# RG-LRU gates as 64x64 quarters in fp32, recurrence gate kept in SBUF, three staging slots for evacuation

## The reference

```python
xh = xc.reshape(B_, N, LRU_HEADS, LRU_HD)          # 8 heads of 64 channels
r = sigmoid(einsum('bnhi,hij->bnhj', xh, wa).reshape(B_, N, W_LRU) + ba)
i = sigmoid(einsum('bnhi,hij->bnhj', xh, wx).reshape(B_, N, W_LRU) + bx)
log_a = (-LRU_C * r) * softplus(-lam)
a = exp(log_a)
b = sqrt(-expm1(2.0 * log_a)) * (i * xc)           # h_t = a_t h_(t-1) + b_t, both directions
```

## Time and profile before

| | us |
|---|---|
| three runs | 788.52, 792.53, 792.26; median 792.26 |
| the profiled execution | 792.91 |
| its span | 790.7 |
| PE busy in the span | 739.8 (94%) |
| DVE, ACT, POOL busy | 526.6, 449.5, 272.5 |
| from gates(0) to gates(19) | 142.37 to 460.12 |
| PE busy in those 317.75 us | 312.90 |
| ACT busy in them | 253.94 |

### The profile page before, as it was taken

The page is one execution under the profiler, slowest core; times in us unless marked ns, Lnnn a source line. Parts: engine busy times, 40 slices in busy tenths (PEclk is TensorE's granted clock), DMA queues, the critical chain, the costliest instruction groups (busy, mean ns, idle before and its releaser), DMA issues.

```text
span 790.7 us, 9934 instructions
## 1 busy us (share of the span) xinstructions
PE 739.8 (94%) x3468; PEld 602.7 (76%) x3468; DVE 526.6 (67%) x811; ACT 449.5 (57%) x743; POOL 272.5 (34%) x321
## 2 busy tenths in 40 slices
PE   3886989999999999999998999899999999999997
PEld 1574767888888887888887877677787888888885
DVE  4377653757998798887995754776646665666522
ACT  4266643699786986787884982234535133534311
POOL 0122335243534274234423345233211134353421
PEclk9796989999999999999999999899999999999999
DMA  8997003334365355345444043254458667968531
GB/s 360 369 325 225 27 28 96 105 97 117 115 182 151 86 157 176 112 141 162 146 130 137 34 127 135 82 160 134 116 194 315 223 205 244 302 202 293 181 116 72
DMA packets 89218, 130.11 MB, mean 165 GB/s; under 512 B 22768, under 2 KB 54128, under 8 KB 87632
## 3 DMA queue, kind: packets, MB, share of 16 engines
q1 hardware_dynamic: 84800, 115.44, 45.1%
q0 software_dynamic: 4368, 14.03, 6.4%
HBM read 91.17 MB, written 38.27 MB: 164 GB/s over the span
## 4 chain that ended last, share of the span: by engine, by line
PE 59%; DVE 14%; issue 7%; ACT 7%; DMA 7%; POOL 4%; SPq 1%; DVEq 0%; ACTq 0%; POOLq 0%
PE bank L1544 19%; PE bank L1546 19%; PE bank L1545 19%; DMA wm<-in_w_mod 3%; DMA pv<-scratch_u 1%; DVE xg L1186 1%; DVE Qb L1301 1%; DVE xc L1129 1%; ACT fbuf L895 1%; DVE spl L1348 1%; POOL xTh L609 1%; ACT bank L878 1%; DVE xTl L1194 1%; DVE Ib L1291 1%; DVE gacc L1129 1%
## 5 line engine op out<-in xcount | busy, mean ns | idle before, releaser
L1544 PE MATMUL bank<-xTh,wh 128*128 128x512 f32 (+1 forms) x592 | 238.2, 402 | 7.2 <-DVE xTl L1194 4.4
L1546 PE MATMUL bank<-xTh,wl 128*128 128x512 f32 (+1 forms) x592 | 231.9, 392 | 0.0
L1545 PE MATMUL bank<-xTl,wh 128*128 128x512 f32 x576 | 227.2, 395 | 0.0
L1544 PEld LDWEIGHTS bank<-xTh,wh 128*128 128x128 f32 x592 | 113.8, 192 | 32.8 <-DVE xTl L1194 6.4
L1546 PEld LDWEIGHTS bank<-xTh,wl 128*128 128x128 f32 x592 | 113.3, 191 | 23.7
L1545 PEld LDWEIGHTS bank<-xTl,wh 128*128 128x128 f32 x576 | 110.2, 191 | 22.6 <-issue 1.2
L1544 PE MATMUL bank<-xTh 128*128 128x512 f32 (+1 forms) x272 | 104.2, 383 | 1.3 <-issue 0.8
L1546 PE MATMUL bank<-xTh,xTl 128*128 128x512 f32 x256 | 99.6, 389 | 0.0
L1545 PE MATMUL bank<-xTl,xTh 128*128 128x512 f32 x256 | 99.6, 389 | 0.0
L911 ACT ACTIVATE ustage<-bank 128x512 f32<-128x512 f32 x56 | 33.1, 592 | 93.0 <-PE bank L1546 76.3
L609 POOL TENSOR_SCALAR sph<-xc 128x512 fp32r<-128x512 f32 (+1 forms) x36 | 27.1, 769 | 121.1 <-PE bank L1546 68.4
(11 more groups left out here) (192 smaller groups left out, 1413.0 us busy)
## 6 DMA issues: line engine op xcount, KB each, us to landing
scratch_u<-ustage SPq DMA_DIRECT2D x72, 256.0 KB, 3.3
wraw<-in_w_in SPq DMA_DIRECT2D x18, 512.0 KB, 4.6
wm<-in_w_mod SPq DMA_DIRECT2D x8, 1024.0 KB, 14.4
xg<-in_x SPq DMA_DIRECT2D x16, 512.0 KB, 9.0
yb<-scratch_y SPq DMA_DIRECT2D x32, 256.0 KB, 3.6
gb<-scratch_u SPq DMA_DIRECT2D x32, 256.0 KB, 5.1
xres<-in_x SPq DMA_DIRECT2D x16, 512.0 KB, 4.7
out<-tout SPq DMA_DIRECT2D x15, 512.0 KB, 3.0
```

The source lines that it names most:

```text
L1544: mm(out, wh_, xh_, start=first, stop=False)
L1545: mm(out, wh_, xl_, start=False, stop=False)
L1546: return mm(out, wl_, xh_, start=False, stop=last)
```

## The change

The gate products are no longer split. `xc` and the raw 64x64 weight blocks (`gwr`, now two buffers) go to PE as fp32, each block a product of its own with 64 rows and 64 columns. Direction d has four: (rows 0-63 to columns 0-63) and (rows 64-127 to columns 64-127) make r; the two blocks of the input gate are written crosswise, rows 0-63 to columns 64-127 and rows 64-127 to columns 0-63. So the input gate's halves are swapped in PSUM, and ACT reads them back with two activations of 64 partitions for each direction. `gates(q+1)` waits for `xc` itself (`s_cv`) and all sigmoids. r is written to a new SBUF tile `rb`, on which exp, tanh and `one_minus_a2` work. `U_SLOTS` is 3. On DVE, `conv(here + 4)` moves from behind the scans of the context step to behind `one_minus_a2` of the next step (s = 1). The splits of `xc` and of the gate weights are gone on POOL and DVE. The weights' high parts stay on ACT as before; `pyo` and `posc2` only change address. `mm` below is one fp32 matmul of the program, which the hardware runs as two instructions.

```diff
-U_SLOTS = 2
+U_SLOTS = 3
...
-        sph = a3.take("sph", [P, 2, CH], f32r)
-        spl = a3.take("spl", [P, 2, CH], f32r)
...
-        gwh = a3.take("gwh", [P, 4, P], f32r)
-        gwl = a3.take("gwl", [P, 4, P], f32r)
-        gwr = a3.take("gwr", [P, 4, 64])
+        gwr = a3.take("gwr", [P, 2, 4, 64])
+        rb = a3.take("rb", [P, 2, CH])
...
             def load_gate_w(t):
-                if t:
-                    pool.wait_ge(s_gwl, 2 * t)
-                g.dma_start(gwr[:], gate_w[t]).then_inc(s_gw, 16)
+                if t >= 2:
+                    pool.wait_ge(s_pg, (NCH + 1) * (t - 1))
+                g.dma_start(gwr[:, t % 2], gate_w[t]).then_inc(s_gw[t % 2], 16)
...
-                if q + 1 < STEPS:
-                    split(q + 1)
...
                 for d in range(2):
-                    r = gr[d][:, 0:n]
-                    a.activation(r, r, ACT.Sigmoid, bias=par_col("lru_ba", 4 * d + t)).then_inc(s_sig, 1)
+                    a.activation(rb[:, d, 0:n], gr[d][:, 0:n], ACT.Sigmoid,
+                                 bias=par_col("lru_ba", 4 * d + t)).then_inc(s_sig, 1)
                 for d in range(2):
                     if q:
                         act.wait_ge(s_st, 2 * (q - 1) + d + 1)
-                    a.activation(Ib[:, d, 0:n], gi_[d][:, 0:n], ACT.Sigmoid,
-                                 bias=par_col("lru_bx", 4 * d + t)).then_inc(s_sig, 1)
+                    for h, other in ((slice(0, 64), slice(64, 128)), (slice(64, 128), slice(0, 64))):
+                        a.activation(Ib[h, d, 0:n], gi_[d][other, 0:n], ACT.Sigmoid,
+                                     bias=par_col("lru_bx", 4 * d + t)[h]).then_inc(s_sig, 1)
...
                 one_minus_a2(q)
-                if q + 1 < STEPS:
-                    split_lo(q + 1)
+                if s == 1:
+                    conv(here + 4)
...
                 if s == 0:
                     conv(here + 3)
-                    conv(here + 4)
...
                 if s == 0:
-                    pe.wait_ge(s_gwl, 2 * t + 2)
-                pe.wait_ge(s_sl, splits_before(q + 1))
+                    pe.wait_ge(s_gw[t % 2], 16 * (t // 2 + 1))
+                pe.wait_ge(s_cv, (NCH + 1) * t + LAST_PIECE[s] + 1)
                 if q:
-                    pe.wait_ge(s_sig, 4 * q)
-                    pe.wait_ge(s_m2, 2 * q)
-                for m in range(4):
-                    d = 0 if s == 0 else m // 2
-                    b = gi_[m // 2] if m % 2 else gr[m // 2]
-                    ins = mm3(b[:, 0:n], gwh[:, m, :], gwl[:, m, :], sph[:, d, 0:n], spl[:, d, 0:n], True, True)
+                    pe.wait_ge(s_sig, 6 * q)
+                w, top, low = gwr[:, t % 2], slice(0, 64), slice(64, 128)
+                for d, c in enumerate(step_chunks(s)):
+                    x = xc_piece(t, c)
+                    mm(gr[d][top, 0:n], w[top, 2 * d], x[top], start=True, stop=True)
+                    mm(gr[d][low, 0:n], w[low, 2 * d], x[low], start=True, stop=True)
+                    mm(gi_[d][low, 0:n], w[top, 2 * d + 1], x[top], start=True, stop=True)
+                    ins = mm(gi_[d][top, 0:n], w[low, 2 * d + 1], x[low], start=True, stop=True)
                 ins.then_inc(s_pg, 1)
```

More of the change, by code:

```diff
@@ L177, in mixer_kernel @@
         Qb = a3.take("Qb", [P, 2, CH])
[L178 to L180 removed]
+        gwr = a3.take("gwr", [P, 2, 4, 64])
+        rb = a3.take("rb", [P, 2, CH])
+        a3.off += 4 * (CH + 2 * 4 * P - 4 * 64)
         MID_BYTES = a3.off - r0 - 4 * (CTX + SEQ)
@@ L201, in mixer_kernel @@
         lsl = past.take("lsl", [P, 2, CH], f32r)
+        pyo = past.take("pyo", [P, CH])
         a4 = Area(mid0, conv0)
@@ L204, in mixer_kernel @@
         ly = a4.take("ly", [P, 2, CH])
-        pyo = a4.take("pyo", [P, CH])
         pdh = a4.take("pdh", [P, CH], f32r)
@@ L238, in mixer_kernel @@
         posr2 = a6.take("posr2", [P, 2, CH])
-        posc2 = a6.take("posc2", [P, CH])
+        posc2 = at("posc2", [P, CH], conv0)
         def col(i, n=1):
@@ L285, in mixer_kernel @@
         s_us = [sem(f"u_stored{b}") for b in range(U_SLOTS)]
-        s_gz, s_gw, s_gwh, s_gwl = sem("gatew_zeroed"), sem("gatew_in"), sem("gatew_hi"), sem("gatew_lo")
+        s_gw = [sem(f"gatew_in{b}") for b in range(2)]
         s_v, s_cv = [sem(f"v_in{b}") for b in range(2)], sem("convolved")
-        s_sh, s_sl, s_pg, s_sig = sem("split_hi"), sem("split_lo"), sem("gates_done"), sem("sigmoids")
+        s_pg, s_sig = sem("gates_done"), sem("sigmoids")
         s_aq, s_exp, s_m2, s_rt = sem("a_and_q"), sem("tanhs"), sem("one_minus_a2"), sem("roots")
@@ L680, in gated_input @@
                 for d, c in enumerate((f, b)):
-                    pool.wait_ge(s_sig, 4 * q + d + 3)
+                    pool.wait_ge(s_sig, 6 * q + 2 * d + 4)
                     I = Ib[:, d, 0:n]
@@ L745, in _ @@
                 here, after = (NCH + 1) * t, (NCH + 1) * (t + 1)
-                if s == NCH and more:
-                    gate_w_hi(t + 1)
                 if s == 0:
                     load_v(here + 4)
-                if q + 1 < STEPS:
-                    split(q + 1)
                 if s == 1 and more:
@@ L931, in decays @@
                     kc = 4 * d + t
-                    act.wait_ge(s_sig, 4 * q + d + 1)
+                    act.wait_ge(s_sig, 6 * q + d + 1)
                     if s == 0 and t or s == 4:
                         act.wait_ge(s_ya, 4 * t if s == 0 else 4 * t + 2)
-                    r = gr[d][:, 0:n]
+                    r = rb[:, d, 0:n]
                     a.activation(Ab[:, d, 0:n], r, ACT.Exp, scale=kn[:, kc:kc + 1]).then_inc(s_aq, 1)
@@ L1248, in _ @@
             lo_group(NCH)
-            def gate_w_lo(t):
-                for i, h in enumerate((slice(0, 64), slice(64, 128))):
-                    dve.wait_ge(s_gwh, 2 * t + i + 1)
-                    v.tensor_tensor(out=gwl[h, :, h], in0=gwr[h], in1=gwh[h, :, h].bitcast(f32),
-                                    op=ALU.subtract).then_inc(s_gwl, 1)
             def conv(p):
@@ L1281, in one_minus_a2 @@
                     dve.wait_ge(s_exp, 2 * q + d + 1)
-                    stt(Qb[:, d, 0:n], Qb[:, d, 0:n], 1.0, gr[d][:, 0:n], ALU.add, ALU.mult).then_inc(s_m2, 1)
+                    stt(Qb[:, d, 0:n], Qb[:, d, 0:n], 1.0, rb[:, d, 0:n], ALU.add, ALU.mult).then_inc(s_m2, 1)
             def scans(q):
@@ L1339, in conv_w_lo @@
                 v.tensor_tensor(out=cwl[:, b], in0=cwraw[:, b], in1=cwh[:, b].bitcast(f32), op=ALU.subtract).then_inc(s_cwlo, 1)
-            def split_lo(q):
-                t, s = divmod(q, NCH + 1)
-                n = CTX if s == 0 else CH
-                pieces = step_chunks(s)[0:1] if s == 0 else step_chunks(s)
-                for d, c in enumerate(pieces):
-                    dve.wait_ge(s_sh, splits_before(q) + d + 1)
-                    v.tensor_tensor(out=spl[:, d, 0:n], in0=xc_piece(t, c), in1=sph[:, d, 0:n].bitcast(f32),
-                                    op=ALU.subtract).then_inc(s_sl, 1)
             w_lo(4)
@@ L1364, in _ @@
             conv(0)
-            gate_w_lo(0)
-            split_lo(0)
             conv(1)
@@ L1373, in _ @@
                         conv(2)
-                if s == NCH and t + 1 < N_LRU:
-                    gate_w_lo(t + 1)
                 for j in convs_in_step(q, 4):
```

25 lines of the change are left out of this document (removed).

## The result

| | before | after |
|---|---|---|
| median of 8 runs each | 791.81 us | 796.67 us (794.22 to 799.64) |
| ratio, 95% interval | | 1.0076 [1.0050, 1.0101] |
| the profiled execution | 792.91 | 799.64 |
| its span | 790.7 | 797.6 |
| from gates(0) to gates(19) | 317.75 | 322.89 |

What follows compares the result with a forecast made beforehand. PE's instruction stream was taken to bound the gate stage. Gates -19.0, edges +8, waits +0.4 and tail +1.2 gave -9.4 us: 792.9 to 783.5, stated as 783; own range 773 to 792, stated range 772 to 798.

Steps and rivals of the forecast that it cites:

- the paragraph on ACT: Gate stage: two more activations a step, 21.6 us against 63.8 us of ACT idle time, costed at nothing.
- ACT takes over the bound: Rival: gates as cheap as forecast, but ACT's 21.6 us do not fit; 6 us of gain lost, 789; 15 in 100.
- the signs that were to show me wrong: PE waiting for `ustage` or sigmoids in many steps, or the time behind step 19 changing by more than 2 us.
- tail: Behind step 19: PE's 4.64 us wait for pooling weights, fetched after a chain through the sigmoids, grows by 1.2 us.
- gates four at once: Gate products: four array quarters run together, 1.72 us for 2.77 a full step, 0.86 for 1.42 a context step; gain 19.0.
- edges: Going into and out of quarters on PE, two a step: 0.4 us a step, 8 us back in all (0 to 14).
- waits ahead of gates(2), gates(12): New PE waits from the moved `conv(here + 4)` and later sigmoids: about 1.4 us in step 1, 0.5 in step 11.
- third slot: Staging: removes ACT waits like the 8.6 us, which cost PE nothing now but pay part of ACT's bill.
- Both bank rivals: Gate quarters: row halves writing one PSUM bank take turns, 830, 13 in 100; row halves never overlap, 876, 4 in 100.
- the rival of dearer edges: Going into and out of quarters costs 0.9 us a step, weights and streams starting anew: +10 us, 793; 8 in 100.
- that of free ones: Rival: the change does all it says and going into and out of quarters costs nothing: 775; no separate chance.
- The holes of steps 9 and 16: PE idle within these steps: step 9 falls from 1.6 to about 0.5 us, step 16 from 3.14 to near 2.7.

Runs made afterwards that it cites:

- e1: Changed kernel with each direction's input gate read by one whole sigmoid, the exchange of halves left out (output not the reference's): 776.26 us, ratio 0.9819.
- e12: Changed kernel with the recurrence gate's sigmoid back in place in PSUM, gates waiting for `one_minus_a2`: 793.92 us, ratio 1.0037.
- e10: As e9, with the recurrence gate's sigmoid in place in PSUM and gates waiting for `one_minus_a2`: 776.64 us, ratio 0.9828.
- e9: Changed kernel with whole input-gate sigmoids, halves of `xc` exchanged by DMA from POOL's queue, `conv(here + 4)` early: 780.15 us, ratio 0.9867.
- e8: As e6, with the recurrence gate in place in PSUM: 785.9 us, ratio 0.9937.
- e6: Changed kernel with whole input-gate sigmoids, halves of `xc` exchanged by DVE copies, `conv(here + 4)` early: 790.8 us, ratio 1.0012.
- e5: Kernel before, with only each input-gate sigmoid cut into two of 64 partitions, no swap: 807.0 us, ratio 1.0209.
- e11: e1 with two staging slots in place of three, exchange of halves also left out: 780.41 us, ratio 0.9872.

## Why the prediction was wrong

**The step that failed is the paragraph on ACT,** "So I cost it at nothing", and the zero was wrong in three ways.
- *The price.* "Two more activations a step are 16 x 1.16 + 4 x 0.75 = 21.6 us". They are 27.1 us (e1). I took a half for another whole one, 0.58 us. But whole ones in a row overlap their neighbour by 0.12 us (length 0.69, 0.57 apart), and halves stand end to end (four in 2.81 us, 0.70 each): 1.70 us a step and not 1.16. The Trainium skill ("ScalarE: Activation LUTs", What ACT_TABLE_LOAD costs) gives the time of an activation of 128 partitions by its columns, and an overlap of about 93 ns between activations in a row. The whole ones here agree (0.12 us); of 64 partitions it says nothing, and the halves don't show the overlap.
- *A second zero,* in the paragraph behind it. "Moving r to SBUF adds no instruction; the exps already cross from PSUM to SBUF. Zero too." The exps start 0.61 us apart on `rb` and 0.57 on PSUM, six such activations a step with the tanh: 4.9 us of ACT (e12 against after), 4.6 (e10 against e9), and with DVE's share, which I had at nothing too, 3 to 6 us of time (e12 against after, e10 against e9, e8 against e6). Together ACT grew by 31.3 us in the stage; 27.1 and 4.9 make 32.0.
- *The consumer.* "Carried from step to step, ACT's debt stays under 2 us, and it may run about 9 us late before the next gates miss a sigmoid ..." ACT's lag rose from 2.0 to 5.8 us in step 5 and 10.8 in step 8. The changed kernel's gates indeed never missed a sigmoid. What ran dry first was another: `cvzl` of a conv unit, on DVE behind `one_minus_a2`, on ACT's tanh. I had asked what PE waits for from ACT by name, and not what stands behind a DVE instruction that waits for ACT. The idle time I offset the debt against (63.8 us) wasn't free either: a late evacuation makes the next conv weights late (7.26 us of ACT's time in step 7), so lateness feeds itself.

The rival "ACT takes over the bound" had the right mechanism, with 6 us and 15 in 100. Of the signs that were to show me wrong, PE's waits for `ustage` or sigmoids in many steps didn't come, though ACT was the cause; the one that came is the tail, changed by more than 2 us. The stated own range of 773 to 792 is also narrower than its terms, whose bounds added end to end give 772 to 799. The halves took 20 us (after against e1), 16 on the kernel before (e5).

**The sum against the runs** (the stage: 322.89 - 303.67 = 19.2 us between after and e1, of which 13.4 are waits of PE, 17.3 against 3.9 us, and 5.8 the lower clock behind them, by PE's busy time of 305.57 against 299.75, 5.75 of it in the stretches of steps 8, 9 and 16). The times of the two profiled executions differ by 26 us and the medians by 20, so single waits of this pair are good to a few us:

| term | forecast | measured |
|---|---|---|
| gates four at once | 1.72 us a full step | 1.72 (turns of 0.43; what the first has more is in the edges) |
| edges | 0.4 us a step | 0.35 |
| waits ahead of gates(2), gates(12) | 1.4, 0.5 | 1.77, 1.08 (0.09 and none in e1) |
| ACT | 0 | 20 us of time |
| third slot | 0 | -15 us in this state, -4 with ACT at ease |
| tail | +1.2 | +3.1 |

- *Both bank rivals are refuted.* Two row halves wrote one bank and one starts 0.01 us behind the other. By the Trainium skill ("TensorEngine Tiling (Array Packing)", Gotcha 1: PSUM Pressure) this shouldn't be. The Trainium skill's "PSUM — Partial Sum Buffer", PSUM bank collisions raise a hardware error, says the same, and beside it that measured collisions were those within one bank and one quadrant of partitions. Here the halves lie in different partitions, and the trace goes with the second. What the prediction calls the "full value" of packing in rows and columns is, on its page, a speedup of 10.6 with 16 tiles.
- *Edges:* 0.35 us, as taken; the rival of dearer edges and that of free ones both fall.
- *Waits:* gates(2) and gates(12) are right in place and near in size, but that is partly luck. The sum gave 0.5 us of it to the halves and 0.9 to the moved piece; the halves cost 1.70 us a step, and without them the moved piece costs 0.09 us at gates(2) (e1). The holes of steps 9 and 16, said to be 0.5 and 2.7, are near that where ACT isn't late (e10: 1.06 and 1.98; e1: 2.29 and 1.54), and 4.05 and 4.30 in the change.
- *Tail:* the chain named (pooling weights) is not the one that showed: in the change the first pooling product has no wait of note, where 5.8 us were forecast. PE waits 3.28 us for ACT's `ustage` and 3.78 for `lq`; with ACT at ease (e1) the pooling wait is 1.29, not 4.64, so the tail got shorter by 2.8 us. Why the pooling weights come earlier I didn't look into, nor the head, which is 1.4 us shorter.
- *Third slot:* of the waits that it removes the prediction said that they "cost PE nothing now but pay part of ACT's bill". The second half was right, but it had no number: 15 us in the state that came about. The zero was wrong by 4 in the state that I had forecast.

The forecast of -9.4 us fits e11, where neither halves nor slot are: -10.1. Its stage is 10.45 us shorter than before (307.30 us), for 10.6 in the sum. Two misses cancel in that: the waits at gates(2) and gates(12), forecast at 1.9 us, are 0.1, and the holes of steps 9 and 16, forecast at 3.2 together, are 5.3.

## What to carry to other kernels

Before adding work to an engine that isn't the bottleneck, follow it to everything that stands behind its consumers in their queues, not only to the waits that name it; an average of 80% busy left no room here, since much of its idle time was spent waiting for things that its own lateness delays. An instruction on half the partitions costs at least a whole one: put an exchange of partitions where data moves anyway or where an engine is idle (a DMA from SBUF to SBUF did it here for 1.3 us of waits, while on ACT the halves cost 20 us of time and the copies on DVE took nearly all of that back). And price a buffer in the state in which it will be needed: the same slot was worth 4 us and 15.
